# A transformer pair on one core: the MLP's input is split before its norm factor is known, and the factor's square multiplies the second matrix's output

## The reference

```python
def rmsnorm(x, g):
    xf = x.astype(jnp.float32)
    y = xf * lax.rsqrt(jnp.mean(xf * xf, axis=-1, keepdims=True) + EPS)
    return (y * g.astype(jnp.float32)).astype(x.dtype)
...
        x = x + merged @ w_out[l]
        h2 = rmsnorm(x, norm2_g[l])
        x = x + jnp.square(jax.nn.relu(h2 @ w_mlp_in[l])) @ w_mlp_out[l]
    return rmsnorm(x, final_g)
```

## Time and profile before

| | us |
|---|---|
| median of 3 runs | 3401.2 (3398.76 to 3404.22) |
| the profiled execution, its time | 3399.34 |
| its span in the trace | 3397.5 |
| TensorE busy | 3241.3 (95%) |
| VectorE busy | 1878.2 (55%) |
| ScalarE busy | 1390.1 (41%) |
| GpSimd busy | 282.9 (8%) |
| mean granted TensorE clock | 0.974 of full |

### The profile page before, as it was taken

One profiled execution on the slowest core, in us unless ns is written; L12 is line 12 of the kernel. 1 busy time (PEld: TensorE's weight loads), 2 busy tenths in 40 slices (PEclk: granted clock), 3 DMA queues, 4 the chain that ended last, 5 costly groups with the idle time before them and its releaser, 6 DMA issues.

```text
span 3397.5 us, 51539 instructions
## 1 busy us (share of the span) xinstructions
PE 3241.3 (95%) x21324; PEld 2907.1 (86%) x21324; DVE 1878.2 (55%) x2467; ACT 1390.1 (41%) x1933; POOL 282.9 (8%) x323
## 2 busy tenths in 40 slices
PE   8999999998899999999898999999999999999998
PEld 7777777767778888887797779999999899999998
DVE  2333333366455578888656884444564644545454
ACT  2222222244243357777541013674434433434343
POOL 0000000021100000000128640000002000000002
PEclk9999999999799999999898998999999999999999
DMA  5222222212235569999553333445555454545553
GB/s 201 87 75 87 75 87 75 87 64 106 81 127 186 192 252 369 372 368 367 218 186 125 123 112 131 162 168 180 211 181 181 159 186 174 186 174 186 186 183 140
DMA packets 80432, 578.85 MB, mean 170 GB/s; under 512 B 8913, under 2 KB 9169, under 8 KB 11218
## 3 DMA queue, kind: packets, MB, share of 16 engines
q1 hardware_dynamic: 78336, 566.27, 45.7%
q10 hardware_dynamic: 1874, 9.34, 0.7%
HBM read 571.37 MB, written 4.19 MB: 169 GB/s over the span
## 4 chain that ended last, share of the span: by engine, by line
PE 82%; DVE 10%; ACT 2%; DMA 2%; POOL 2%; issue 2%; SPq 0%; ACTq 0%; POOLq 0%; DVEq 0%
PE PG L591 13%; PE PG L589 13%; PE PG L592 13%; PE PG L619 10%; PE PG L916 4%; PE PG L917 4%; PE PG L918 4%; PE PX L689 3%; PE PG L560 3%; PE PX L956 2%; PE PX L957 2%; PE PX L958 2%; DVE work L2055 1%; DMA ring<-weights 1%; DVE ring_r L498 1%
## 5 line engine op out<-in xcount | busy, mean ns | idle before, releaser
L498 DVE TENSOR_TENSOR ring_r<-ring,work_r 128x1024 fp32r<-128x1024 f32 x532 | 627.7, 1221 | 343.7 <-ACT work_r L491 338.9
L491 ACT ACTIVATE work_r<-ring 128x1024 fp32r<-128x1024 f32 x532 | 534.5, 1053 | 577.8 <-PE PG L592 419.9
L592 PE MATMUL PG<-work_r,ring_r 128*128 128x256 f32 x2624 | 738.0, 281 | 0.0
L498 DVE TENSOR_TENSOR ring_r<-ring,C_r 128x1024 fp32r<-128x1024 f32 x372 | 440.2, 1225 | 269.5 <-ACT C_r L491 265.0
L491 ACT ACTIVATE C_r<-ring 128x1024 fp32r<-128x1024 f32 x372 | 373.6, 1052 | 475.5 <-PE PG L592 401.7
L592 PEld LDWEIGHTS PG<-work_r,ring_r 128*128 128x128 f32 x2624 | 497.4, 190 | 0.0
L619 PE MATMUL PG<-HT,ring 128*128 128x256 f32 x1728 | 436.8, 391 | 0.0
L589 PE MATMUL PG<-work_r,C_r 128*128 128x256 f32 x1312 | 368.1, 281 | 20.5 <-DVE HT_r L509 11.2
L589 PE MATMUL PG<-work_r 128*128 128x256 f32 x1312 | 368.1, 281 | 0.0
L619 PEld LDWEIGHTS PG<-HT,ring 128*128 128x128 f32 x1728 | 312.4, 191 | 56.0 <-issue 10.6
L592 PE MATMUL PG<-XT_r,ring_r 128*128 128x256 f32 x1152 | 325.1, 282 | 0.0
(11 more groups left out here) (463 smaller groups left out, 5671.6 us busy)
## 6 DMA issues: line engine op xcount, KB each, us to landing
ring<-weights SPq DMA_DIRECT2D x536, 1024.0 KB, 4.8
XT<-xT SPq DMA_DIRECT2D x4, 512.0 KB, 10.5
residual<-XT ACTq DMA_DIRECT2D x4, 512.0 KB, 2.6
XT<-residual ACTq DMA_DIRECT2D x1, 2048.0 KB, 10.8
result<-YT SPq DMA_DIRECT2D x4, 512.0 KB, 2.6
C<-constants ACTq DMA_DIRECT2D x1, 1608.0 KB, 8.4
work<-gate_up ACTq DMA_DIRECT2D x1, 1024.0 KB, 15.1
work<-lora ACTq DMA_DIRECT2D x1, 512.0 KB, 11.7
```

Source lines behind the costliest of these rows:

```text
L491: act.activation(w_high(u)[:, c], ring[:, u % RING, c], ACT.Copy).then_inc(w_hi, 1)
L498: dve.tensor_tensor(ring_r[:, u % RING, c], ring[:, u % RING, c], w_high(u)[:, c].bitcast(F32), ALU.subtract).then_inc(w_lo, 1)
L592: last = pe.matmul(o, wl, high[:, k, :], start=False, stop=(n == kts - 1), skip_group_check=True)
```

## The change

The factor r of a token commutes with a matrix, and relu(r h)² = r² relu(h)². The changed kernel therefore splits the input of the MLP without r, each tile as soon as its residual is complete, inside the `wo2` stage; r² (the reciprocal of mean square plus eps, no root) is worked out once during block 0 and multiplies every output tile of the second matrix before it is added to `XT`.

```diff
         M_HI = rounded(gates_at, KT)
-        HID = cube(area(KT * T, gates_at + KT * T), KT)
-        HID_LO = rounded(gates_at + KT * T, KT)
-        HID_HI = rounded(gates_at + 2 * KT * T, KT)
+        HID = cube(area(KT * T, gates_at), KT)
+        HID_LO, HID_HI = rounded(gates_at, KT), HT_r
+        H2_HI, H2_LO = rounded(gates_at + 2 * KT * T, KT), rounded(gates_at + KT * T, KT)
...
+        R2 = YT[:, 2, :]
...
                 split_unit(U0["wo2"] + t, B0["wo2"] + t, M_HI, HT_r, before=fours("merged", t == 0))
-            norm(3)
-
-            def block_of_hidden(i):
+
+            def block_of_hidden(i, first=False):
                 u, use = U0["mlp"], B0["mlp"]
                 for t in range(KT):
-                    split_unit(u + t, use + t, M_HI, HT_r, more=i * 32, free=i * 8,
-                               before=fours("h2", t == 0))
+                    split_unit(u + t, use + t, H2_HI, H2_LO, more=i * 32, free=i * 8,
+                               before=(lambda k: pe.wait_ge(h2_lo, k + 1)) if first and t == 0 else None)
+                    if first and t == 1:
+                        norm(3)
...
-            with pe.Fori(0, 3) as i:
+            block_of_hidden(0, first=True)
+            with pe.Fori(1, 4) as i:
                 block_of_hidden(i)
-            block_of_hidden(3)
...
@@ scalar @@
                     split_high(act, U0["wo2"] + t + 2)
                 if t:
                     wait_taken(act, B0["wo2"] + t - 1)
+                    act.activation(H2_HI[:, t - 1, :], XT[:, t - 1, :], ACT.Copy,
+                                   scale=vec("norm2", t - 1)).then_inc(h2_hi, 1)
                     square(3, t - 1)
-            root(3)
             split_high(act, U0["mlp"] + 1)
-            for q in range(4):
-                act.wait_ge(s_h, 3 * KT + 4 * q + 4)
-                four_high(act, M_HI, HT, q)
...
@@ vector @@
             for t in range(KT):
                 add_tile(U0["wo2"] + t, B0["wo2"] + t, t)
-                if t < KT - 1:
-                    split_low(dve, U0["wo2"] + t + 2)
-            norm(3, "norm2", low=lambda q: four_low(dve, HT_r, HT, M_HI, q, X0["h2"] + q),
-                 second=U0["mlp"] + 1)
+                dve.wait_ge(h2_hi, t + 1)
+                dve.scalar_tensor_tensor(H2_LO[:, t, :], XT[:, t, :], vec("norm2", t), H2_HI[:, t, :].bitcast(F32),
+                                         ALU.mult, ALU.subtract).then_inc(h2_lo, 1)
+                split_low(dve, U0["wo2"] + t + 2)
...
+                    if first and n == KT - 1:
+                        dve.wait_ge(s_sqsum, 3)
+                        dve.tensor_scalar(RS[:, :], PX[:, 0, 0:T], 1.0 / D, 1e-6, ALU.mult, ALU.add).then_inc(s_r2, 1)
+                        dve.wait_ge(s_r2, 1)
+                        dve.reciprocal(R2, RS[:, :]).then_inc(s_r2, 1)
+                        dve.wait_ge(s_r2, 2)
                     if not (last and n + 2 >= 2 * KT):
                         split_low(dve, U0["mlp"] + n + 2, more=i * 32)
...
                         dve.wait_ge(unit_done, i * 32 + (U0["mlp"] + n + 1))
-                        x = XT[:, n - KT, :]
-                        dve.tensor_tensor(x, x, PG[:, use % BANKS, 0:T], ALU.add).then_inc(free_bank(use), 1)
+                        x, y = XT[:, n - KT, :], YT[:, n % 2, :]
+                        dve.tensor_tensor(y, PG[:, use % BANKS, 0:T], R2, ALU.mult).then_inc(s_scaled, 1)
+                        dve.wait_ge(s_scaled, i * KT + (n - KT + 1))
+                        dve.tensor_tensor(x, x, y, ALU.add).then_inc(free_bank(use), 1)
```

More of the change, by code:

```diff
@@ L335, in build @@
             "products", "log", "softplus", "sums", "exponent", "weights", "values", "out"))
-        s_relu = sem("mlp_relu")
+        s_relu, s_scaled = sem("mlp_relu"), sem("mlp_out_scaled")
+        h2_hi, h2_lo, s_r2 = sem("mlp_in_high"), sem("mlp_in_low"), sem("mean_square_inverse")
         c_zero, s_yb = sem("s5_zeroed"), sem("glu_out")
@@ L512, in build @@
         X0, _n = {}, 0
-        for _name, _fours in [("y", 4), ("h1", 4), ("s5", 2), ("ya", 2), ("yb", 2), ("yc", 2), ("merged", 4),
-                              ("h2", 4)]:
+        for _name, _fours in [("y", 4), ("h1", 4), ("s5", 2), ("ya", 2), ("yb", 2), ("yc", 2), ("merged", 4)]:
             X0[_name] = _n
@@ L544, in _ @@
             for q in range(4):
-                sp.wait_ge(s_h, 4 * KT + 4 * q + 4)
+                sp.wait_ge(s_h, 3 * KT + 4 * q + 4)
                 sp.dma_start(out[:, 4 * q:4 * q + 4, :], YT[:, 4 * q:4 * q + 4, :]).then_inc(s_out, 16)
@@ L1550, in hidden_high, with block_of_hidden @@
                 act.activation(HID_HI[:, t, :], HID[:, t, :], ACT.Copy).then_inc(hid_hi, 1)
-            def block_of_hidden(i, last=False):
+            def block_of_hidden(i, first=False, last=False):
                 for n in range(2 * KT):
@@ L1560, in block_of_hidden @@
                         act.wait_ge(unit_done, i * 32 + (U0["mlp"] + n + 1))
+                        if first and n == 0:
+                            act.wait_ge(s_squsd, 4 * KT)
                         if n >= 2:
@@ L1570, in block_of_hidden @@
                         square(4, n - KT - 1)
-            with act.Fori(0, 3) as i:
+            block_of_hidden(0, first=True)
+            with act.Fori(1, 3) as i:
                 block_of_hidden(i)
@@ L1576, in _ @@
             square(4, KT - 1)
-            root(4)
+            root(3)
         @block.vector
@@ L2195, in block_of_hidden @@
                         dve.wait_ge(unit_done, i * 32 + (U0["mlp"] + n + 1))
-                        x = XT[:, n - KT, :]
-                        dve.tensor_tensor(x, x, PG[:, use % BANKS, 0:T], ALU.add).then_inc(free_bank(use), 1)
-            with dve.Fori(0, 3) as i:
+                        x, y = XT[:, n - KT, :], YT[:, n % 2, :]
+                        dve.tensor_tensor(y, PG[:, use % BANKS, 0:T], R2, ALU.mult).then_inc(s_scaled, 1)
+                        dve.wait_ge(s_scaled, i * KT + (n - KT + 1))
+                        dve.tensor_tensor(x, x, y, ALU.add).then_inc(free_bank(use), 1)
+            block_of_hidden(0, first=True)
+            with dve.Fori(1, 3) as i:
                 block_of_hidden(i)
```

2 lines of the change are left out of this document (1 added, 1 removed).

## The result

| | before | changed |
|---|---|---|
| median of 6 runs, us | 3401.9 (3396.6 to 3408.2) | 3493.2 (3489.5 to 3496.9) |
| ratio | 1 | 1.0268 [1.0254, 1.0283] |
| profiled execution, span | 3397.5 | 3491.7 |
| mean granted TensorE clock | 0.974 | 0.964 |

What follows compares the result with a forecast made beforehand. TensorE, busy 95% of the span, was taken as the bound. Stalls 60.2, clock 19.6 and small terms 4.7, less the 12.5 gain, made 72.0 us more: 3473 us, slower by 2.1%, range 3450 to 3492.

Steps and rivals of the forecast that it cites:

- The gain of 12.5 us: Between `wo2` and the MLP: TensorE no longer waits for the norm, 12.5 us saved, clock loss after the pause included.
- ones-matmul: Small term: the matmul with ones, formerly in the norm's pause, now stands between MLP units 1 and 2; 0.71 us added.
- The circle in the `wo2` stage: VectorE's next weight split queues behind ScalarE's tile copy, itself behind splits awaiting a unit's end; units 2 to 15 wait, 60.2 us.
- A stall of 4.3 us: In `wo2`, TensorE's wait per unit from ScalarE's splits, copy, VectorE's low parts and hops: 4.3 us, 14 times.
- rival 2: In `wo2`, GpSimd's addition slips in before VectorE's weight split; each stall 0.72 us longer, 10 in all: 3483 us. Chance 0.13.
- 1.4 us of clock a stall: One stretch of half clock after each of 14 `wo2` stalls, 1.4 us lost each, 19.6 us in all.
- rival 3: Two low-clock stretches instead of one after each `wo2` stall: 14 x 1.6 us more, 3495 us. Chance 0.07.
- Small terms: Ones-matmul 0.7, mean and reciprocal in block 0 2.3, clock behind that 1.2, last output 0.5: 4.7 us added.
- the pause at the second matrix of block 0: Mean and reciprocal delay hidden tiles 14 and 15: 2.3 us more on a 0.70 wait, plus 1.2 for clock.
- The last output: Second matrix: each output's extra instruction is hidden for 63 of 64; the last, before the final norm, adds 0.5 us.
- the table load: The square root's table is loaded ahead of the last root, while ScalarE waits; no cost was counted.
- Rival 4: No stalls in `wo2`, if ScalarE's copy is done before the next unit ends: 3393 us, faster by 0.23%. Chance 0.03.

Runs made afterwards that it cites:

- The two orders: Two edits of the changed kernel, each alone: ScalarE's tile copy ahead of its weight splits (3390.7 us), or VectorE's weight split ahead of its wait for that copy (3392.3 us).
- the run with 38 matmuls: Changed kernel plus 38 matmuls of no use behind each of `wo2` units 1 to 14, filling TensorE's pauses; 3473.7 us, 1.0211 of the kernel before.
- copy first: Changed kernel with ScalarE's copy and square of tile t-1 ahead of the weight splits of unit t+2 in `wo2`; 3390.7 us, 0.9969 of the kernel before.
- weights first: Changed kernel with VectorE's weight split of unit t+2 ahead of its wait for ScalarE's copy of tile t; 3392.3 us, 0.9978 of the kernel before.

## Why the prediction was right or wrong, point by point

- **The gain of 12.5 us**: right. From VectorE's last addition of the `wo2` stage to ScalarE's first relu of the MLP it is 2651.08 less 2630.92, 20.16 us, in the kernel before, and 2742.54 less 2734.91, 7.63 us, in the changed one: 12.53 less. The relu before, then the addition and the relu in the changed kernel:

```profile
2651.08 0.36 ACT L1564 ACTIVATE SQ<-PG 128x256 f32<-128x256 f32 x1
```
```profile
2734.91 0.42 DVE L1812 TENSOR_TENSOR XT<-XT,PG 128x256 f32<-128x256 f32 x1 [2.10 <-PE PG L593]
...
2742.54 0.36 ACT L1565 ACTIVATE SQ<-PG 128x256 f32<-128x256 f32 x1
```

  TensorE goes from `wo2` unit 15 to MLP unit 0 without a pause. In the kernels without the 14 pauses the length in the table is only 9.7 to 11.9 shorter than before. Inside it lie also the ones-matmul, a low stretch of 3.4 or 6.8 us after the last pause before the stage, which the trace of before lacks, and a pace of the first matrix that no term foresaw (last section).
- **The circle in the `wo2` stage**: right, in each step, the number of stalls (14) and its first and last unit. The two orders are the proof of it.
- **A stall of 4.3 us**: this step failed in part. It is 4.83 of pause and 0.26 behind it at the full clock, 5.09; 14 x 0.79 = 11.1 us. Of this 0.53 a stall is the contention that stood as rival 2, with a chance of 0.13 and a price of 0.72; 0.08 is the copy, 0.49 for 0.41; the rest is the start after the pause, priced at 0.1. The argument against that rival was that VectorE's pairs took 2.36 with GpSimd active or not. In the `wo2` stage of before, VectorE's instruction had always begun first, by 0.15 us. Here GpSimd's addition begins first, by 0.05 us. And elsewhere the trace of before has what the rows lacked: a weight split of 1.65 us, where nearly all others take 1.22, beside an addition of GpSimd that had begun first (there are two such splits):

```profile
1779.91 1.65 DVE L498 TENSOR_TENSOR ring_r<-ring,C_r 128x1024 fp32r<-128x1024 f32 x1
...
1778.86 1.61 POOL L2263 TENSOR_TENSOR YT<-YT,work 128x256 f32<-128x256 f32 x1
```

  The rule of the Trainium skill cited beside the rival ("SBUF — State Buffer", section "Who interferes with whom"), that the first to start wins, is borne out in both directions, by GpSimd's 1.66 and VectorE's 2.89. I should have applied it to the order of arrival that I had worked out myself. 14 x 0.53 = 7.4 us.
- **1.4 us of clock a stall**: this is the other step that failed. It is 13.02 - 10.82 = 2.2 us, by the run with 38 matmuls; 14 x 0.8 = 11.2 us. I had taken one low stretch of about 3.4 us for each, from the pause of 3.31; the pause of 3.59, with its 6.6 us at low clock, was the nearer row for a stall of over 4 us, and it was used as a bound only (and half of 6.6 is 3.3, not 3.0). The low stretches lasted 6.8 us in 11 of 14 stalls and 3.4 in three, each of them with its beginning inside the pause, where it costs nothing. This is rival 3 in most stalls, not in all.
- Together: 14 x 7.29 = 102.1 against 79.8 forecast, 22.3 us more, half by the stall and half by the clock. With that the sum would have been 3495, 2 above the median. The rivals 2 and 3 were treated as excluding each other; they came together, and the range, which took in only the first, ended 1 us short.
- **Small terms**: the pause at the second matrix of block 0 is 2.93 for 0.70 (+2.2, forecast +2.3). The clock behind it was taken too low: the low stretch lasts until 6.05 us after the pause, which at half the clock is about 3 us, an estimate, for the forecast's 1.2 and at most 1.5; in copy first and weights first it is one of 3.4 us. Blocks 1 to 3 have 0.7 as before. The ones-matmul costs 0.43 for 0.71: the unit in which it stands takes 6.08 us for 5.65. The last output costs 0.46 (forecast 0.5), the table load nothing. The other 63 outputs of the second matrix are hidden.
- **Rival 4**, the case without stalls, was priced at 3393; the two kernels that are this case measured 3390.7 and 3392.3.

## What to carry to other kernels

Where each engine runs in its written order, price a new instruction by what it waits for and by what stands behind it, not by its length: 0.9 us of work on two engines that were half idle cost 102 us, because a semaphore wait was put ahead of the work that the bottleneck engine needed next. Put the urgent work (here the weights) ahead of the wait, and the work that is not needed for a stage behind it. A pause of TensorE can cost more than its length: here one of 4.83 us brought 2.2 more by the clock. For this rhythm of pauses the row of the longest earlier pause, with its long low stretch, would have been the better price than that of the shorter one; whether this holds elsewhere no run here tells.

## What the runs showed that I had not expected

- The clock after a pause depends on more than the length of that pause. 13 pauses of 2.60 us, with the same work of TensorE between them, were followed by a low stretch four times; pauses of 4.30 always, by 3.4 or 6.8 us of it; pauses of 4.83 always, mostly by 6.8. On average that cost about 0.5, 1.9 and 2.2 us a pause. Between the pauses of 2.60 TensorE also had 19 matmuls more to make, so these three don't differ in length alone.
- VectorE, not only GpSimd, can be held up where the two meet: 0.53 us of an addition of 0.72.
- TensorE's jump back in the loop over blocks, 3.0 to 3.3 us where no matmuls were added, took two pauses of 5.9 and 6.1 us together with 532 matmuls more ahead of the loop, and of 4.8 and 4.9 us with 266. That it is the jump is argued from its place: the kernel before, whose loop holds blocks 0 to 2, has such a pause behind blocks 0 and 1 (3.31 and 3.17), the changed one, whose loop holds blocks 1 to 3, behind blocks 1 and 2 (3.18 and 2.97), and neither at the third border between blocks, where no loop goes back. The profile puts these pauses down to VectorE's weight split, but this begins 5.65 us after the one before it there, as in other units without a pause. No run here tells why the jump takes what it takes.
- A unit of the MLP has not the same length in both kernels. In the first matrices the relus come every 5.73 us before and every 5.65 in the changed kernel, 1.1 us less over block 0; in the second matrices of blocks 0 and 2 the outputs come every 5.55 us before and every 5.65 now. The cause is not shown.
